# A Mamba-2 scan by tile with rows, taps and SiLU ahead of the outputs, D x on VectorE, and a new order of weights and scalings in the heads

## The reference

```python
xbc, conv_new = causal_dwconv(xbc, conv_buf, p['ssm_conv_w'][j], p['ssm_conv_b'][j])   # 4 taps
xbc = jax.nn.silu(xbc)
xs, bm, cm = split_cols(xbc, [D_A, G_A * N_A, G_A * N_A])
dt = jax.nn.softplus(dt + p['ssm_dt_bias'][j])
# per chunk: cum = cumsum(dt * a)
y = einsum('bign,bjgn->bijg', cb, bb) * decay @ (x * dt)         # inside the chunk
y = y + einsum('bign,bghpn,bigh->bighp', cb, h, jnp.exp(cum))    # from the state
h_new = h * exp(cum[:, -1]) + einsum('bjgn,bjgh,bjghp->bghpn', bb, exp(cum[:, -1:] - cum), x * dt)
y = (y + p['ssm_d'][j][:, None] * xs).reshape(bsz, t, D_A) * jax.nn.silu(z)
y = rms_norm(y.reshape(bsz, t, G_A, D_A // G_A), ...)            # over groups of 512
```

## Time and profile before

| | |
|---|---|
| median of 3 runs | 2446.7 us (2445.29 to 2447.96) |
| profiled execution | 2445.45 us |
| its span | 2443.9 us |
| TensorE busy | 2403.4 us, 98% |
| VectorE busy | 1266.1 us, 52% |
| ScalarE busy | 927.6 us, 38% |
| mean granted clock of TensorE | 0.997 |
| scan by tile (440 to 640 us): TensorE, VectorE, ScalarE busy | 186.0, 149.8, 114.8 us of 200 |

### The profile page before, as it was taken

How to read it: one execution, slowest core, us unless ns; L and a number is a source line. 1 busy time by engine, 2 the same in 40 slices (tenths; PEclk the granted TensorE clock), 3 DMA queues, 4 the chain that set the end, 5 groups by cost and what they waited for, 6 DMA issues and landing times.

```text
span 2443.9 us, 52860 instructions
## 1 busy us (share of the span) xinstructions
PE 2403.4 (98%) x21601; PEld 2376.7 (97%) x21601; DVE 1266.1 (52%) x1850; ACT 927.6 (38%) x1369; POOL 13.9 (1%) x50
## 2 busy tenths in 40 slices
PE   9999999999999999999999999999999999999998
PEld 9999999998999999999999999999999989999998
DVE  5442444777576564433444442444788865442443
ACT  4221223556355543222233221223777744221232
POOL 1000000000000000000000000000000000000000
PEclk9999999999999999999999999999999999999999
DMA  4232333332422232332232332232222223332231
GB/s 142 86 108 69 90 90 85 84 101 72 115 76 61 72 87 86 98 91 78 88 93 78 89 113 65 86 99 76 73 70 70 66 65 91 88 112 61 86 101 48
DMA packets 396034, 208.32 MB, mean 85 GB/s; under 512 B 10015, under 2 KB 393110, under 8 KB 395894
## 3 DMA queue, kind: packets, MB, share of 16 engines
q1 hardware_dynamic: 390502, 202.64, 28.8%
q10 hardware_dynamic: 5392, 3.72, 0.5%
HBM read 200.88 MB, written 5.45 MB: 84 GB/s over the span
## 4 chain that ended last, share of the span: by engine, by line
PE 82%; DVE 6%; ACT 4%; DVEq 2%; ACTq 2%; issue 1%; DMA 1%; SPq 0%
PE PD L2014 68%; PE PD L2044 10%; DVE wlo L1191 1%; DVE c_xl L1707 1%; DMA EP<-cum_rows 1%; DVEq L1708 1%; ACT L673 1%; DVE c_xl L1683 0%; DVEq L1685 0%; PE PM L2418 0%; ACT whi L516 0%; PE PM L2409 0%; DVE c_bw L1668 0%; ACTq L998 0%; ACT L506 0%
## 5 line engine op out<-in xcount | busy, mean ns | idle before, releaser
L516 ACT ACTIVATE whi<-raw 128x1024 fp32r<-128x1024 f32 (+4 forms) x348 | 381.4, 1096 | 1095.6 <-PE PD L2014 992.0
L2014 PE MATMUL PD<-XH,whi 128*128 128x272 f32 x2880 | 596.3, 288 | 0.0
L2014 PE MATMUL PD<-XL,whi 128*128 128x272 f32 x2880 | 594.5, 288 | 0.3 <-DVE XL L1229 0.3
L2014 PE MATMUL PD<-XH,wlo 128*128 128x272 f32 x2880 | 593.8, 287 | 0.0
L2014 PEld LDWEIGHTS PD<-XL,whi 128*128 128x128 f32 x2880 | 452.8, 189 | 0.6 <-DVE XL L1229 0.6
L2014 PEld LDWEIGHTS PD<-XH,whi 128*128 128x128 f32 x2880 | 451.7, 188 | 0.4 <-issue 0.4
L2014 PEld LDWEIGHTS PD<-XH,wlo 128*128 128x128 f32 x2880 | 450.4, 189 | 0.0
L2014 PE MATMUL PD<-AL,whi 128*128 128x272 f32 x1408 | 290.7, 288 | 0.0
L2014 PE MATMUL PD<-AH,whi 128*128 128x272 f32 x1408 | 290.6, 288 | 0.0
L2014 PE MATMUL PD<-AH,wlo 128*128 128x272 f32 x1408 | 289.8, 287 | 0.0
L1191 DVE TENSOR_TENSOR wlo<-raw,whi 128x1024 fp32r<-128x1024 f32 (+4 forms) x182 | 227.3, 1249 | 74.4 <-ACT whi L516 62.7
(11 more groups left out here) (428 smaller groups left out, 2435.4 us busy)
## 6 DMA issues: line engine op xcount, KB each, us to landing
raw<-in_ffn_w_gu SPq DMA_DIRECT2D x176, 512.0 KB, 3.8
raw<-in_ffn_w_down SPq DMA_DIRECT2D x32, 768.0 KB, 4.7
raw<-in_ab_w_in SPq DMA_DIRECT2D x44, 512.0 KB, 3.9
raw<-in_ffn_w_down SPq DMA_DIRECT2D x32, 640.0 KB, 4.2
raw<-in_c_w_in SPq DMA_DIRECT2D x32, 512.0 KB, 4.0
LM<-cum_rows SPq DMA_DIRECT2D x8, 512.0 KB, 4.9
raw<-in_ab_w_out SPq DMA_DIRECT2D x16, 256.0 KB, 2.8
raw<-in_ab_w_out SPq DMA_DIRECT2D x8, 512.0 KB, 3.6
```

Of the source, the lines that this page charges most:

```text
L516: A(whi[ps % 2][:, 0:k, :], raw[ps % 4][:, 0:k, :], ACT.Copy).then_inc(S["hi_ready"], 1)
L2014: last = mm(PD[:, 2 * (ps % 2) + s, 0:HT], wt[ps % 2][:, r, :], x[:, r, s * HT:(s + 1) * HT], start=(p == 0 and q == 0), stop=(p == 2 and ...
```

## The change

- **D x** leaves TensorE: the matmuls with DDG go, and with them DDG and its eight scalings. VectorE's `output` becomes `output_read` and `output_gate`; `output_read` multiplies EP by the state part for frames from 128 on, then computes XX * D + PSUM in one scalar_tensor_tensor, then adds the first product for frames from 128 on.
- **EP** is loaded and exponentiated over all 544 frames, not from frame 128; its load is issued directly behind that of LM and ahead of the next weights.
- **Scan, VectorE**: `taps(4 + m)` comes directly after `row(4 + m)`, ahead of add_square and the outputs.
- **Scan, ScalarE**: the SiLU table load and `conv_silu` come ahead of the second weights, `z_silu` behind them.
- **Last tile**: order rebuilt on TensorE, VectorE and ScalarE.
- **Heads**: in GLA, ScalarE does rstd(h-2) ahead of the second weights, VectorE pre and cumulate ahead of low(h, 2); kd is made ahead of qe; in HGRN2, weights(h, 3) come ahead of the sigmoid table load and near; the ends `last_gla` and `last_hgrn` have a new order of gates, far, near, states and low halves.

```diff
             def decay_rows / spread_rows
-                    sp.dma_start(EP[e * PA:(e + 1) * PA, CH:T], cum_rows[2 * j + e:2 * j + e + 1, CH:T].broadcast_to([PA, T - CH])).then_inc(S["ep_landed"], 16)
+                    sp.dma_start(EP[e * PA:(e + 1) * PA, :], cum_rows[2 * j + e:2 * j + e + 1, :].broadcast_to([PA, T])).then_inc(S["ep_landed"], 16)
...
                 elif b >= 8 and b % 2 == 0:
                     decay_rows(b // 2 - 3)
-                elif b >= 8:
                     spread_rows(b // 2 - 3)
...
 ScalarE, last tile
             square(j - 2)
+            silu_set()
+            conv_silu(4 + j)
             weights(uy + 1)
-            square(j - 1)
-            silu_set()
             z_silu(j)
             differences(j)
             weights(uy + 2)
-            conv_silu(4 + j)
-            weights(uy + 3)
             logs_set()
             decays(j)
+            weights(uy + 3)
+            weights(uy + 4)
             spreads(j)
-            weights(uy + 4)
+            square(j - 1)
             weights(uy + 5)
+            weights(uy + 6)
             square(j)
-            weights(uy + 6)
             state_rows(0)
...
 ScalarE, heads
                     if gla:
                         gate_logits(h)
+                    if gla and h >= 2:
+                        rstd(h - 2)
                     weights(h, 2)
-                    if h >= 2:
+                    if not gla and h >= 2:
                         rstd(h - 2)
...
 ScalarE, last_hgrn
                 turned(7)
+                far(7)
                 silu_set()
                 out_hi(6)
                 take_g(7)
-                far(7)
-                near(7)
                 weights(8, 2)
                 weights(8, 3)
+                near(7)
...
 VectorE
-                TT(y, EP[:, :], PM[:, 0:2, :].rearrange("p s t -> p (s t)")[:, 0:T], ALU.add)
+                STT(y, XX[:, j % 2, :], DCOL[:, j:j + 1], PM[:, 0:2, :].rearrange("p s t -> p (s t)")[:, 0:T], ALU.mult, ALU.add)
+                dve.drain()
+                TT(y[:, CH:T], y[:, CH:T], ep, ALU.add)
                 dve.drain().then_inc(S["y_read"], 1)
...
 VectorE, last tile
+            y_low(0)
+            y_low(1)
             gate_row(j)
-            lo(uy + 1)
             y_low(2)
             y_low(3)
-            taps(4 + j)
+            lo(uy + 1)
+            inputs(j)
+            part(0)
             lo(uy + 2)
-            part(0)
-            inputs(j)
+            output_read(j - 1)
             lo(uy + 3)
             part(1)
             states(j)
             masked(j)
-            add_square(j - 1)
             part(2)
             lo(uy + 4)
-            output(j)
+            add_square(j - 2)
+            output_gate(j - 1)
             part(3)
             lo(uy + 5)
-            add_square(j)
+            output_read(j)
+            add_square(j - 1)
+            output_gate(j)
             part(4)
             lo(uy + 6)
+            add_square(j)
...
 VectorE, last_gla and last_hgrn
-                for m in range(3, 6):
+                gated_lo(3)
+                gated(7)
+                for m in range(4, KT):
                     gated_lo(m)
                 low(4, 9)
-                gated(7)
-                for m in range(6, KT):
-                    gated_lo(m)
...
                 levels(7)
-                states(7)
                 part(0)
                 low(8, 2)
+                states(7)
                 part(1)
...
 TensorE, last tile
             j = KT - 1
-            for r in range(4):
-                out_rows(0, r, r + 1, True)
-            out_rows(1, 0, 4)
+            out_rows(0, 0, 1, True)
+            out_rows(0, 1, 2, True)
             turn(j)
-            out_rows(2, 0, 2)
+            out_rows(0, 2, 3, True)
+            out_rows(0, 3, 4, True)
+            out_rows(1, 0, 3)
             products(j)
-            out_rows(2, 2, 4)
+            out_rows(1, 3, 4)
+            out_rows(2, 0, 4)
             out_rows(3, 0, 4)
             outputs(j)
```

More of the change, by code:

```diff
@@ L196, in build @@
         DROW = place("DROW", [HA], w)
-        DDG = [at(f"DDG{g}", [4, P], raw_at[2 * g + 1] + 8 * P * 4) for g in range(2)]
         LMS = at("LMS", [HA, TS], raw_at[0] + 8 * P * 4)
@@ L403, in _ @@
                     decay_rows(b // 2 + 5)
-                elif b < 6:
                     spread_rows(b // 2 + 5)
@@ L1060, in heads @@
                         take_g(h - 1)
+                        weights(h, 3)
                         sigmoid_set()
                         near(h - 1)
-                        weights(h, 3)
                         take_f(h)
@@ L1116, in last_gla @@
                 gate(6)
-                for m in range(3, 6):
+                for m in range(3, 7):
                     gated_hi(m)
+                gate(7)
                 weights(4, 9)
-                gate(7)
-                for m in range(6, KT):
-                    gated_hi(m)
+                gated_hi(7)
             def last_hgrn():
@@ L1430, in skip_columns @@
                     dve.tensor_copy(DCOL[e * PA:(e + 1) * PA, :], DROW[e * PA:(e + 1) * PA, e:HA:2])
-                dve.drain()
-                for j in range(KT):
-                    TSC(DDG[j // 4][:, j % 4, :], ident[:, :], DCOL[:, j:j + 1], None, ALU.mult)
             def dt_columns():
@@ L1503, in masked, with output_read @@
                 dve.drain().then_inc(S["lm_ready"], 1)
-            def output(j):
+            def output_read(j):
                 dve.wait_ge(S["y_psum"], j + 1)
@@ L1563, in _ @@
                 row(4 + m, ux + 2 * m)
+                taps(4 + m)
                 if m == KT - 1:
-                    y_low(0)
-                    y_low(1)
+                    break
                 if m >= 2:
                     add_square(m - 2)
-                output(m - 1)
-                if m < KT - 1:
-                    taps(4 + m)
+                output_read(m - 1)
+                output_gate(m - 1)
                 if m == KT - 2:
@@ L1690, in decayed @@
                         dve.wait_ge(S["q_made"], j + 1)
+                    dve.wait_ge(S["kd_exp"], j + g0 + 1)
+                    TT(kd[:, 0:T], kd[:, 0:T], k_of(j), ALU.mult)
+                    dve.drain().then_inc(S["kd_ready"], 1)
                     dve.wait_ge(S["e1_ready"], j + g0 + 1)
@@ L1799, in heads @@
                     units(h, 0)
-                    low(h, 2)
                     if gla:
@@ L1803, in heads @@
                         cumulate(h)
+                    low(h, 2)
+                    if gla:
                         if h >= 2:
@@ L2291, in outputs @@
                 pe.wait_ge(S["lm_ready"], j + 1)
-                halves = [slice(e * PA, (e + 1) * PA) for e in range(2)]
                 for c in range(NC):
-                    cs = slice(c * CH, (c + 1) * CH)
-                    for e, es in enumerate(halves):
-                        mm(PM[es, 0, cs], XD[:, c, es], LM[:, e, c, :], start=True, stop=False)
-                    for es in halves:
-                        mm(PM[es, 0, cs], DDG[j // 4][:, j % 4, es], XX[:, j % 2, cs], start=False, stop=True)
-                for e, es in enumerate(halves):
-                    mm(PM[es, 1, 0:TS], XD[:, NC, es], LMS[:, 2 * j + e, :], start=True, stop=False)
-                for es in halves:
-                    last = mm(PM[es, 1, 0:TS], DDG[j // 4][:, j % 4, es], XX[:, j % 2, TP:T], start=False, stop=True)
+                    for e in range(2):
+                        es = slice(e * PA, (e + 1) * PA)
+                        mm(PM[es, 0, c * CH:(c + 1) * CH], XD[:, c, es], LM[:, e, c, :], start=True, stop=True)
+                for e in range(2):
+                    es = slice(e * PA, (e + 1) * PA)
+                    last = mm(PM[es, 1, 0:TS], XD[:, NC, es], LMS[:, 2 * j + e, :], start=True, stop=True)
                 last.then_inc(S["y_psum"], 1)
```

12 lines of the change are left out of this document (6 added, 6 removed).

## The result

| | before | changed |
|---|---|---|
| median | 2446.8 us (2445.29 to 2447.96) | 2426.81 us (2425.95 to 2428.79) |
| profiled execution, its span | 2445.45, 2443.9 us | 2426.13, 2424.6 us |
| TensorE busy | 2403.4 us | 2394.0 us |

The ratio is 0.9917, with a 95% interval of 0.9905 to 0.9929: about 20 us less, where 18.5 were forecast. One of the ten executions of e1 took 10399.67 us and is left out of its ratio.

What follows compares the result with a forecast made beforehand. TensorE, busy 2403.4 of 2443.9 us, was taken as the bound. Savings of 14.7 us (scan), 2.1 (GLA heads and gates) and 1.7 (HGRN2 heads) make 18.5 off 2446.7: 2428.2 us, range 2423.5 to 2435.5.

Steps and rivals of the forecast that it cites:

- VectorE's replay: Scan: VectorE worked forward from tile 0, at 15.3 or 16.2 us a tile, giving times for XD and the products.
- the new wait before the mean: End of the scan: TensorE would wait some 2.2 us for VectorE's last square, with the mean at 606.8.
- the signs: Listed trace marks of a right forecast, among them small waits of 0.2 to 1.7 us at state products from tile 3.
- The price of the added product: Scan outputs on VectorE: a product of 416 elements on Y, 0.58 us and a drain, 0.70 together.
- TensorE's tile: Scan: without its waits and D x, a tile on TensorE could be 16.1 us long, and was 18.1.
- The price of 1.0 us a tile: Scan: D x's matmuls, counted start to start, take 1.0 us of TensorE a tile, 8.0 for 8 tiles.
- The turn waits: Scan: TensorE's waits for ScalarE's SiLU before the turns of tiles 1 to 6 go, 8.0 of 9.0 us; the first stays.
- EP's load: Scan: behind LM it lands some 4 us after XD; ScalarE wants it some 5 us after XD.
- the terms for refilling: GLA heads and gates: refilling the pipe raises the turns' 0.9 us to 1.2, and GOL's 0.8 less 0.1 to 0.9.
- Head 1's take_f: HGRN2 head 1: weights wait for unit (1,1), so take_f comes 0.9 us later, of which 0.65 reaches the next sum.
- Rival 3: HGRN2 heads: weights wait for TensorE's unit in all seven heads, slower than before from 2.6 us each; chance 0.02, in part 0.04.
- Rival 2: Scan: VectorE slower, a hidden wait of 1 us in tiles 1 to 7 given on in full, 2435 us; chance 0.17.

Runs made afterwards that it cites:

- e1: The kernel before with D x moved to VectorE and DDG and its matmuls gone, every order as before: 2448.11 us, ratio 1.0005.
- e3: The changed kernel with the GLA and HGRN2 heads and their ends in the order of before: 2430.10 us, ratio 0.9934.
- e5: e1 with VectorE's taps ahead of add_square and the outputs: 2442.14 us, ratio 0.9981.
- e9: e1 with both the taps ahead of the outputs and EP's load behind that of LM: 2437.29 us, ratio 0.9957.
- e2: The changed kernel with D x given back to TensorE and EP again from frame 128, all new orders kept: 2431.78 us, ratio 0.9939.
- e11: The changed kernel with weights(h, 3) behind the sigmoid's table load and near again in the HGRN2 heads: 2426.99 us, ratio 0.9914.
- e6: e1 with the load of EP directly behind that of LM, taps still behind the outputs: 2441.22 us, ratio 0.9977.
- e7: The changed kernel with one more VectorE step of 416 elements and a drain in each output: 2431.92 us, ratio 0.9940.
- e10: The changed kernel measured again, unedited: 2426.05 us, ratio 0.9910.
- e4: The changed kernel with the second mean and its transpose behind three of the four rows of unit 6: 2426.81 us, ratio 0.9919.

## Why the prediction was right

**The sum.** Forecast were 14.7 us for the scan, 2.1 for the GLA heads and gates, 1.7 for the HGRN2 heads. The stages show 13.5, 1.3 and 2.5 in the changed kernel, and 14.85 for the scan in e3, where the clock did not fall. The rest of the 19.3 us between the two profiled executions is 1.0 at the start, which differs between executions by more than that, and 1.0 behind the heads, which is not the change's: e1, e5 and e9, with the heads as before, are 1.0 us shorter there too, and e2 and e11, with the new order, only 0.3. Of the 2.5 us in the HGRN2 heads some 1.5 are a fall of the clock that did not come (see the clock below); without it they would be 1.0 where 1.7 was forecast.

**VectorE's replay.** XD was forecast at 485.4, 501.1, 517.8, 534.1, 550.4 and 568.3. Shifted by the 0.98 us by which tile 0's turn came earlier, it ran at 485.40, 500.89, 517.50, 533.76, 550.10 and 567.79. VectorE's tile was put at 15.3 or 16.2 us and is 15.49 or 16.26; the new wait before the mean at 2.2 and is 1.87; the mean at 606.8 and came at 606.40 with the shift. The three small waits at the products (0.21, 0.20, 0.84) are those that the signs named. The STT took 0.77 us for 0.78. The price of the added product came out for a weaker reason than stated: the 0.58 that the prediction calls an SBUF step is the row EP<-PM,EP, which reads PSUM. The new product reads SBUF (Y<-Y,EP) and took 0.59.

**TensorE's tile** was put at 16.1 us and is 15.82. The sum was 0.3 us too high; the likeliest term is the refilling of the pipe behind the two waits, which no run separates. It had no effect, since VectorE sets the pace.

**D x.** The price of 1.0 us a tile was right (0.98 in e2 against the changed kernel). That all 8.0 us "lie on TensorE's path" is true only with the new order: alone they gave nothing (e1). The prediction's sum has both, and so came out; a reader who had credited D x with 8 us and the order with 7 would be misled. The order brings 15 us without D x, and D x 5 on top of it.

**The turn waits.** The prediction took as their cause the SiLU's place behind the second high half, which waits for TensorE. For the kernel before that holds in the main. ScalarE there, ahead of the turn at 504.34:

```profile
494.89 0.55 ACT L765 ACTIVATE EP<-EP 128x416 f32<-128x416 f32 x1 [3.35 <-DMA EP<-cum_rows]
...
501.16 1.06 ACT L516 ACTIVATE whi<-raw 128x1024 fp32r<-128x1024 f32 x1 [3.20 <-PE PD L2044]
...
503.53 0.63 ACT L708 ACTIVATE XX<-CV 128x512 f32<-128x512 f32 x1
```

and all waits of the SiLU for the taps:

```profile
ACT XX L708 <- DVE CV L1379: 1.9, 3, 1.4
```

Four of the seven turn waits are 1.02 or 1.03 us with no wait for the taps, the other three 1.17, 1.32 and 2.40 with 0.16, 0.31 and 1.39 of it: 7.1 of the 9.0 us are the cause that the prediction names, 1.9 are the taps. What it did not see is how little room VectorE's way round the tile had, with the taps behind the outputs and, ahead of them, a low half that waited for ScalarE's high half behind EP's load (3.35 us above). With D x on VectorE that way is the longer one: in e1 the SiLU waits 5.3 us for the taps and the turns 12.5. **EP's load was treated as a cost to be checked; with D x on VectorE its new place was a gain of 5 to 7 us** (e5 to e9, e1 to e6), some of it through falls of the clock that did not come. The replay did not price that: it assumed no wait at the low half, which is true only with the new place. Whether the gain is as large with the taps ahead and the SiLU moved, no run shows; none takes back EP's place alone.

**The clock.** No term of the sum has it. The new wait before the mean cost 1.4 us more than its length, and the wait in c_open, 1.1 us shorter, no longer brought a fall with it, which gave 1.4 to 1.6 us back. The two cancel, which is luck; either alone would have left the forecast inside its range.

**GLA.** Forecast 2.1 us, measured 1.3 to 1.9 against e3. The turns wait no more and GOL neither (1.7 us of waits), so the terms for refilling (0.5 us together) were probably too high.

**HGRN2 heads.** Head 1's take_f was to come 0.9 us later against the start of the stage: it stands at 1731.84 where 1746.58 - 15.76 = 1730.82 would be unchanged (15.76 us is the shift at the start of the stage, 0.99 + 13.48 + 1.29), 1.0 us. The loss at the gate of head 1 is 1.0, where 0.65 was taken. The third unit of c_open was to start 1.7 us earlier against the start of the stage: 1983.08 - 1966.18 - 15.76 = 1.1 us, or 2.0 without head 1's loss. Rival 3 did not come: in heads 2 to 7 the weights held nothing up.

**Rival 2** (a hidden wait of 1 us a tile) did not come either; e7 shows that most of it would have been paid, as the rival said: 4.7 us of 5.6.

## What to carry to other kernels

Before work is moved from one engine to another, follow the loop from one tile to the next through every queue: here 8 us of matmuls could leave TensorE without any gain, since the way through VectorE, a high half and a small load that was issued late was nearly as long as TensorE's, and the work moved made it the longer one. With the new order TensorE and VectorE were nearly equally long (15.8 and 16.3 us a tile), and then no step is worth its length: 7.8 us of matmuls more cost the scan 3.2 (e2 against e3), 5.6 us of VectorE more cost it 4.7 (e7). A change that leaves a wait of some 2 us on TensorE should be counted with a fall of the clock as a possible extra.

## What the runs showed of the hardware

Behind some waits TensorE ran for about 3 us at 1.2 GHz (granted clock 0.50), and the two such falls that were measured cost 1.4 and 1.6 us. The thirteen profiles (before, changed, eleven experiments) hold these waits of TensorE from 100 us on:

| wait, us | clock fell | did not fall |
|---|---|---|
| 2.66 to 3.47 | 12 | 0 |
| 1.80 to 2.58 | 9 | 9 |
| up to 1.49 | 0 | all |

In the middle row the same wait at the same place came out both ways: before the mean 1.80, 1.80 and 1.87 us fell (e11, e10, changed) and 1.81 did not (e3); in c_open 2.43 and 2.45 fell (e2, e4) and 2.39 and 2.40 did not (changed, e10); e6 has two turn waits of 1.84 us, one of each kind. What else decides is open, and it moves a result by as much as the smaller edits here.
